# A first norm summed by token, x fetched first, and two of the last four token groups scaled on GpSimd

## The reference, cut to what matters

```python
h = jnp.concatenate([meta, x], axis=1)                 # 528 x 1024
xn = rmsnorm(h, g_mix_pre[l])                          # h * rsqrt(mean(h*h) + 1e-6) * g
proj = xn @ w_in[l]                                    # columns: q, k, v, r, a_low, u, z_gla, z_ssm
...
log_a = jax.nn.log_sigmoid(a_low @ w_gate_up[l] + b_gate[l]) / GATE_TAU
...                                                    # gated linear attention, state-space layer, FFN
...                                                    # second block: attention, convolution, mixture of experts
x = x + gt2 * hierarchical_moe(...)
return rmsnorm_2(x, final_norm_g)                      # 512 x 1024, the output
```

## Time and profile before

| | |
|---|---|
| median of 3 runs | 1752.39 us (1750.7 to 1757.69) |
| the profiled execution's own time | 1752.41 us |
| its span | 1750.6 us |
| TensorE matmul busy | 1661.9 us, 95% |
| VectorE busy | 1192.2 us, 68% |
| ScalarE busy | 736.7 us, 42% |
| GpSimd busy | 329.5 us, 19% |
| granted TensorE clock, mean | 0.979 |

### The profile page before, as it was taken

One profiled execution on the slowest core, in us unless ns is written; L12 is line 12 of the kernel. 1 busy time (PEld: TensorE's weight loads), 2 busy tenths in 40 slices (PEclk: granted clock), 3 DMA queues, 4 the chain that ended last, 5 costly groups with the idle time before them and its releaser, 6 DMA issues.

```text
span 1750.6 us, 20019 instructions
## 1 busy us (share of the span) xinstructions
PE 1661.9 (95%) x8290; PEld 1328.2 (76%) x8290; DVE 1192.2 (68%) x1584; ACT 736.7 (42%) x975; POOL 329.5 (19%) x191
## 2 busy tenths in 40 slices
PE   6999899899999998999999998999999998999997
PEld 4878787777888886888887897878755776777775
DVE  5979768872434337953466446968965657899998
ACT  5253445444422243221222224334476237677774
POOL 1000011214100001600000000433401004355452
PEclk8999999999999998999999998999999999999999
DMA  5535213433322233444334421222210105999995
GB/s 221 187 116 168 71 61 111 138 110 109 121 96 94 91 131 118 168 168 176 135 146 170 157 107 56 108 83 97 97 48 1 72 1 222 383 387 383 385 364 188
DMA packets 59643, 264.54 MB, mean 151 GB/s; under 512 B 21648, under 2 KB 22288, under 8 KB 33056
## 3 DMA queue, kind: packets, MB, share of 16 engines
q1 hardware_dynamic: 34896, 159.10, 24.9%
q0 software_dynamic: 15184, 99.90, 14.5%
q10 hardware_dynamic: 9472, 4.26, 0.9%
HBM read 239.80 MB, written 23.44 MB: 150 GB/s over the span
## 4 chain that ended last, share of the span: by engine, by line
PE 73%; DVE 17%; ACT 6%; DMA 2%; issue 1%; POOL 1%; ACTq 0%; SPq 0%; DVEq 0%; POOLq 0%
PE bank L377 72%; DVE bank L2378 3%; DVE wsplit L1699 2%; DVE wsplit L2644 2%; DMA ring<-in_wmoe,indices 1%; ACT wsplit L1049 1%; DVE parts L2644 1%; ACT parts L1636 1%; DVE products_early L1795 1%; POOL wsplit L1699 1%; DVE block_out L2686 0%; DVE x_in L1726 0%; PE bank L854 0%; DMA x_in<-in_xT 0%; DVE products_early L1814 0%
## 5 line engine op out<-in xcount | busy, mean ns | idle before, releaser
L377 PE MATMUL bank<-h_high,wsplit 128*128 128x512 f32 (+1 forms) x1056 | 329.1, 391 | 11.4 <-DVE h_low L2221 4.9
L1699 DVE TENSOR_TENSOR wsplit<-ring,wsplit 128x2048 fp32r<-128x2048 f32 x77 | 178.8, 2322 | 158.5 <-ACT wsplit L1049 158.3
L1049 ACT ACTIVATE wsplit<-ring 128x2048 fp32r<-128x2048 f32 x98 | 187.1, 1909 | 202.0 <-PE bank L377 190.8
L377 PEld LDWEIGHTS bank<-h_high,wsplit 128*128 128x128 f32 x1056 | 199.9, 193 | 55.1 <-DVE h_low L2313 5.4
L377 PE MATMUL bank<-xn_high,wsplit 128*128 128x512 f32 (+1 forms) x832 | 220.1, 352 | 11.0 <-DVE xn_low L1730 8.1
L377 PE MATMUL bank<-h_low,wsplit 128*128 128x512 f32 (+1 forms) x528 | 204.5, 387 | 0.0
L377 PEld LDWEIGHTS bank<-xn_high,wsplit 128*128 128x128 f32 x832 | 147.4, 193 | 33.9 <-DVE xn_low L1730 8.1
L377 PE MATMUL bank<-f_high,wsplit 128*128 128x512 f32 (+1 forms) x576 | 171.8, 375 | 1.1 <-DVE wsplit L1699 1.1
L377 PE MATMUL bank<-xn_low,wsplit 128*128 128x512 f32 (+1 forms) x416 | 144.9, 348 | 0.0
L1699 POOL TENSOR_TENSOR wsplit<-ring,wsplit 128x2048 fp32r<-128x2048 f32 x21 | 97.4, 4640 | 176.8 <-ACT wsplit L1049 176.7
L377 PEld LDWEIGHTS bank<-f_high,wsplit 128*128 128x128 f32 x576 | 105.3, 188 | 21.1 <-DVE wsplit L1699 1.3
(11 more groups left out here) (508 smaller groups left out, 3309.3 us busy)
## 6 DMA issues: line engine op xcount, KB each, us to landing
ring<-in_W SPq DMA_DIRECT2D x122, 1024.0 KB, 4.8
weights_out<-prep SPq DMA_DIRECT2D x8, 864.0 KB, 5.5
prep<-weights_out_early POOLq DMA_DIRECT2D x8, 576.0 KB, 3.1
xslot<-zeros SPq DMA_DIRECT2D x7, 516.0 KB, 5.1
block<-xslot SPq DMA_DIRECT2D x6, 516.0 KB, 12.0
yslot<-block_out SPq DMA_DIRECT2D x6, 512.0 KB, 8.7
prep<-turns_early POOLq DMA_DIRECT2D x8, 288.0 KB, 2.4
x_in<-in_xT SPq DMA_DIRECT2D x4, 528.0 KB, 7.5
```

The source lines that it names most:

```text
L377: return g.matmul(o, l, r, start=first, stop=last_, skip_group_check=True)
L1049: g.activation(wst[:, side(n), 0, :], ringt[:, n % RING, :], ACT.Copy).then_inc(*a.sig(("high", n)))
L1699: g.tensor_tensor(wst[:, side(n), 1, :], ringt[:, n % RING, :], hi, SUB).then_inc(*t.sig(("low", n), ("released", n)))
```

## The change

The x loads are issued first, then the constants, ring load 0, the vectors, ring load 1, `wal`, `wgu`, ring load 2. The squares are summed over k on VectorE; TensorE then sums over the partitions with the squares as the stationary operand, so that the sum of a token lies on one partition: 128x5 instead of 128x528. Root and reciprocal are taken of that small tile, and TensorE spreads it again into two PSUM banks, from which the scaling reads it. Small products (`keep_busy`) stand before, between and behind. The first weight unit is split in two halves, its low part by VectorE and GpSimd; the second unit's high part goes between the x parts on ScalarE and its low part directly behind the scaling loop on VectorE. The root's table is loaded at the start. At the end, groups 0 and 1 are scaled on GpSimd in two steps.

```diff
 tensor:
+            def keep_busy(n):
+                for _ in range(n):
+                    t = mm(idle[:, 0:128], ones, ident, True, True)
+                t.then_inc(*p.sig(("free", "idle")))
             p.wait_ge(cst_landed, 16)
-            for k in range(8):
-                p.wait_ge(*at("sq", k))
-                mm(ba, ones, sq[:, k % 4, 0:512], k == 0, k == 7)
-                mm(bb[:, 0:16], ones, sq[:, k % 4, 512:NT], k == 0, k == 7)...
+            keep_busy(4)
+            b = fresh("ms")
+            p.wait_ge(*at("ms", "square"))
+            for m, lo in enumerate((0, 128, 256, 384, 400)):
+                t = mm(b[:, m:m + 1], sq[:, 0, lo:lo + 128], ones[:, 0:1], m == 0, m == 4)
+            t.then_inc(*p.sig(("ms",)))
+            keep_busy(2)
+            b, b2 = fresh("ms", "scale"), fresh("ms", "tail")
+            p.wait_ge(*at("inverse", "ms"))
+            for m in range(4):
+                mm(b[:, 128 * m:128 * m + 128], rt5[:, m:m + 1].to_broadcast([128, 128]), ident, True, True)
+            mm(b2[:, 0:16], rt5[:, 4:5].to_broadcast([128, 128]), ident[:, 112:128], True, True)...
+            keep_busy(8)
 linear:
-                p.wait_ge(*at("low", n))
+                p.wait_ge(*at("low_part", 0) if n == 0 else at("low", n))
+                        if n == 0 and k == 4:
+                            p.wait_ge(*at("low_part", 1))
 scalar:
+            g.activation(small[:, 40:41], small[:, 40:41], ACT.Sqrt)          # loads the table
-                    a.wait_ge(*at("summed", k - 4))
-                g.activation(sq[:, k % 4, :], HT0[:, k, :], ACT.Square)...
-            high(0)
-            root(("ms", 1), rst[:, 512:NT], 1024, 16)
-            root(("ms", 0), rst[:, 0:512], 1024, 512)
+                    a.wait_ge(*at("sq_added", k - 3))
+                g.activation(sq[:, 1 + (k - 1) % 3 if k else 0, :], HT0[:, k, :], ACT.Square)...
+            g.activation(rt5, banks.at("ms")[:, 0:5], ACT.Sqrt, scale=1.0 / 1024, bias=eps)...
+            high_part(0, 0)
+            high_part(0, 1)
             for k in range(8):
                 g.activation(xnh[:, k, :], HT0[:, k, :], ACT.Copy)...
+                if k in (3, 5):
+                    high_part(1, k // 4)
-            next_high("k", 0)
 vector:
-            low(v, g, 0)
-            inverse(rst[:, 512:NT], "root", "ms", 1)
-            inverse(rst[:, 0:512], "root", "ms", 0)
+            for k in range(1, 8):
+                v.wait_ge(*at("sq", k))
+                g.tensor_tensor(sq[:, 0, :], sq[:, 0, :], sq[:, 1 + (k - 1) % 3, :], ADD)...
+            g.reciprocal(rt5, rt5)...
+            low_part(v, g, 0, 0)
             for k in range(9):
-                    g.scalar_tensor_tensor(out=HT0[:, k, :], in0=HT0[:, k, :], ..., in1=rst, ...)
+                    for w, c in (("scale", slice(0, 512)), ("tail", slice(512, NT))):
+                        g.scalar_tensor_tensor(out=HT0[:, k, c], in0=HT0[:, k, c], ...,
+                                               in1=banks.at("ms", w)[:, 0:c.stop - c.start], ...)
+            next_low("k", 0)                     # was behind ssm_angle
 finish(m):
                 g.reciprocal(ss[:, 4 + m:5 + m], ss[:, m:m + 1]).then_inc(*v.sig(("y_inverse", m)))
+                if m < 2:
+                    return
 gpsimd:
+            low_part(q, g, 0, 1)                 # ahead of the odd x parts
+            for m in range(2):                   # at the very end
+                q.wait_ge(*at("y_inverse", m))
+                g.tensor_scalar(HT[:, m, 0:1024], HT[:, m, 0:1024], ss[:, 4 + m:5 + m], None, MUL)...
+                q.wait_ge(*q.own())
+                g.tensor_tensor(HT[:, m, 0:1024], HT[:, m, 0:1024], ROWS[:, 1, :], MUL)...
 sync:
-            g.dma_start(vt[:, :], vecs)...; g.dma_start(ct[:, :], cst[:, 0:NCST])...
             for i in range(4):
                 g.dma_start(HT0[:, 2 * i:2 * i + 2, :], xT[:, 2 * i:2 * i + 2, :])...
+            g.dma_start(ct[:, :], cst[:, 0:NCST])...
+            load(0)
+            g.dma_start(vt[:, :], vecs)...
+            load(1)
             g.dma_start(walt, wal)...
             g.dma_start(wgut[0:16, :], wgu)...
-            loads(0, RING)
+            load(2)
```

More of the change, by code:

```diff
@@ L264, in program @@
         rx, z4 = small[:, 16:20], small[:, 20:24]
-        rt4 = small[:, 44:48]
+        rt4, rt5 = small[:, 44:48], small[:, 48:53]
         hh, hl = tile("h_high", 0, 8, 512, dt=F32R), tile("h_low", 14336, 8, 512, dt=F32R)
@@ L1075, in root, with high_part @@
                 g.activation(o, b[:, 0:w], ACT.Sqrt, scale=1.0 / dim, bias=eps).then_inc(*a.sig(("free", *name), ("root", *name)))
+            def high_part(n, z):
+                w = slice(1024 * z, 1024 * z + 1024)
+                a.wait_ge(*landed(n))
+                g.activation(wst[:, side(n), 0, w], ringt[:, n % RING, w], ACT.Copy).then_inc(*a.sig(("high_part", n, z), ("high", n)))
+            a.wait_ge(*at("one"))
+            g.activation(small[:, 40:41], small[:, 40:41], ACT.Sqrt).then_inc(*a.sig())
             for k in range(8):
@@ L1080, in scalar @@
                 if k > 3:
-                    a.wait_ge(*at("summed", k - 4))
-                g.activation(sq[:, k % 4, :], HT0[:, k, :], ACT.Square).then_inc(*a.sig(("sq", k)))
-            high(0)
+                    a.wait_ge(*at("sq_added", k - 3))
+                g.activation(sq[:, 1 + (k - 1) % 3 if k else 0, :], HT0[:, k, :], ACT.Square).then_inc(*a.sig(("sq", k)))
             a.wait_ge(cst_landed, 16)
-            root(("ms", 1), rst[:, 512:NT], 1024, 16)
-            root(("ms", 0), rst[:, 0:512], 1024, 512)
+            a.wait_ge(*at("ms"))
+            g.activation(rt5, banks.at("ms")[:, 0:5], ACT.Sqrt, scale=1.0 / 1024, bias=eps).then_inc(*a.sig(("free", "ms"), ("root", "ms")))
+            high_part(0, 0)
+            high_part(0, 1)
             for k in range(8):
@@ L1715, in scaled @@
                 g.scalar_tensor_tensor(out=o, in0=x, scalar=gain, in1=rs, op0=MUL, op1=MUL).then_inc(*v.sig((name, k)))
-            low(v, g, 0)
-            inverse(rst[:, 512:NT], "root", "ms", 1)
-            inverse(rst[:, 0:512], "root", "ms", 0)
+            g.memset(small[:, 40:41], 1.0).then_inc(*v.sig(("one",)))
+            for k in range(1, 8):
+                v.wait_ge(*at("sq", k))
+                v.wait_ge(*v.own())
+                g.tensor_tensor(sq[:, 0, :], sq[:, 0, :], sq[:, 1 + (k - 1) % 3, :], ADD).then_inc(*v.sig(("sq_added", k), ("ms", "square")))
+            v.wait_ge(*at("root", "ms"))
+            g.reciprocal(rt5, rt5).then_inc(*v.sig(("inverse", "ms")))
+            low_part(v, g, 0, 0)
             v.wait_ge(vecs_landed, 16)
-            v.wait_ge(*v.own())
+            for k in range(4):
+                v.wait_ge(x_landed[k], 16)
+            v.wait_ge(*at("ms", "scale"))
             for k in range(9):
                 if k < 8:
-                    v.wait_ge(x_landed[k // 2], 16)
-                    g.scalar_tensor_tensor(out=HT0[:, k, :], in0=HT0[:, k, :], scalar=vec("g_mix_pre")[:, k:k + 1], in1=rst,
-                                           op0=MUL, op1=MUL).then_inc(*v.sig(("xn_value", k)))
+                    for w, c in (("scale", slice(0, 512)), ("tail", slice(512, NT))):
+                        g.scalar_tensor_tensor(out=HT0[:, k, c], in0=HT0[:, k, c], scalar=vec("g_mix_pre")[:, k:k + 1],
+                                               in1=banks.at("ms", w)[:, 0:c.stop - c.start], op0=MUL, op1=MUL).then_inc(
+                            *v.sig(("xn_value", k), ("free", "ms", w)))
                 if k % 2:
@@ L1824, in vector @@
             g.tensor_scalar(q1, q1, PI_IN, -PI_IN, ALU.min, MAX).then_inc(*v.sig(("ssm_angle",)))
-            next_low("k", 0)
             v.wait_ge(*at("ssm_abs"))
```

29 lines of the change are left out of this document (21 added, 8 removed).

## The result

The changed kernel is slower, where I had forecast 5.7 us faster: 1759.57 us median (22 runs, 1748.41 to 1765.84) against 1753.09 for the kernel before (22 runs, 1749.81 to 1759.53). The ratio is 1.0036, 95% interval 1.0025 to 1.0047: some 6 us slower.

What follows compares the result with a forecast made beforehand. Bound: mostly TensorE, with a latency chain in front of its dense stretch. Span 1750.6 - 9.3 (front) + 3.6 (tail) = 1744.9; time 1752.4 - 5.7 = 1746.7 us, range 1741.5 to 1752.5, forecast chance 0.45.

Steps and rivals of the forecast that it cites:

- The front, -9.3: Kernel start up to the gates: earlier x, smaller norm and faster scaling gain 9.3 us, between 6.6 and 10.8.
- the pair of k without GpSimd's interference: Scaling loop: with the scale read from PSUM, VectorE stops waiting for GpSimd's split; a pair takes 2.45 us instead of 3.04.
- TensorE's wait of 1.3 us: At the gates, TensorE, 10.8 us early, waits about 1.5 us for banks VectorE frees, 8.0 early with 1.3 slack.
- my fear for the clock level: Front, TensorE: less sure that the granted level has risen from 0.50 by 20 us; staying low costs 3.0 us.
- From 110 on everything 9 us early: After the front, unchanged code to the tail: the 9.3 us gained in front are kept throughout.
- The tail, +3.6: Last 12 us: finishing groups 0 and 1 on GpSimd delays the final stores, losing 3.6 us, between 1.4 and 4.4.
- The one-operand multiply of 128x1024: Tail, GpSimd: one of two steps per group, taken as 1.05 us, between a copy's 1.0 and the two-operand 2.3.
- Three stores after group 1, 5.6 us: Tail, SP: stores go in group order, so three start only after group 1; the end comes 5.6 us later.
- Rival (4): Tail: contention slows GpSimd's products to 6.5 us each, delaying three stores; 1755.2 us, slower than before; chance 0.08.
- (1): Tail and gate banks: GpSimd gets the port first twice, banks free early enough; -10.8 + 1.4, 1743.0 us; chance 0.24.
- (2): Front, TensorE: small products do not lift the clock, first 6 us at 1.2 GHz; 7.4 early, 1748.6 us; chance 0.13.
- (3): Front, loads: x lands no earlier, at 12.2, as transfers share engines; front gains 6.6, 1749.4 us; chance 0.10.

Runs made afterwards that it cites:

- the five unpadded kernels with the new front: Kernels whose TensorE program is that of the change, without extra 1x1 products; state-space stage averages 445.9 us, against 441.8 with the old front.
- the front alone: The change with the last four groups finished on VectorE as in the kernel before; 1750.59 us, ratio 0.9977, and 1747.71 us, 0.9973, when repeated.
- the front alone with shifted code: New front, old tail, with 16, 32 or 48 extra 1x1 TensorE products, or 13 keep-busy products removed; ratios 0.9950, 0.9939 (repeated 0.9934), 0.9949, 0.9948.

## Why the prediction was wrong

**The front, -9.3: right, in part by luck.** x, the scale at 16.7, the pair of k without GpSimd's interference, VectorE's 9.5 (I had 8.0) and TensorE's wait of 1.3 us all came as written. The measured shift is 9.1 us at 44 and 9.7 at 186 us. The wait came out right because two errors cancelled: at the gates VectorE is 8.8 us early (forecast 8.0) and TensorE 12.1 (forecast 10.8). Small errors: the constants land at 9.5 (10.7 forecast), and my fear for the clock level was needless even without the idle products. With all but one of them gone the first 60 us read

```profile
0.00:60.00 60.00, 46.25 (x301) 42.84 (x302) 45.16 (x152) 25.33 (x42) 10.95 (x11) 1.00 0.68 260
```

level 1.00 throughout, and the kernel is 9.1 us early at 43.8 all the same.

**"From 110 on everything 9 us early": wrong.** I carried 9.3 us over 1600 us of unchanged code. In the state-space stage the five unpadded kernels with the new front lose 445.9 - 441.8 = 4.1 us, to 3 us more gaps and to the low level behind them. 9.3 - 4.1 is 5.2, the front alone measured 4 (0.9977 and 0.9973). That the loss does not come from the work of the front is shown by the front alone with shifted code, whose ratios of 0.9934 to 0.9950 are 9 to 12 us.

**The tail, +3.6: the step that failed.** It measured +9.8 alone. Its lower end should read 1.5 (1752.1 - 1750.6), not 1.4, which changes nothing. Three terms, by the trace of after:
- The one-operand multiply of 128x1024 was priced at 1.05 us, near the copy. It takes 2.85 beside VectorE's additions from PSUM, which keep their pace (1.48 us for two), more than the two-operand product, 2.34. Two of them add 3.6 us to the GpSimd chain; the collisions gave some 1.2 back, since one multiply was stretched by 0.95 where the value taken had 2.1 for both. Group 1 was ready 11.7 us after the first reciprocal started instead of 9.3: 2.4 us.
- Three stores after group 1, 5.6 us: right, 1742.3 to 1747.7 is 5.4.
- The end of the program: no term at all in the sum. It comes 9.2 us after GpSimd's last instruction, not 5.6: 3.6 us.
The forecast's 3.6 with these two additions of 2.4 and 3.6 is 9.6.

The Trainium skill ("VectorE: DVE Perf Modes", "The DRAIN you can't avoid") says that the DRAINs which the runtime puts before and behind a program take a constant 12 ns or so on all five engines. The closing DRAINs here stand at a line of the kernel itself, and no run shows whether that sentence means them. Taken for them the figure would be far off: they took 9120 to 18063 ns on GpSimd in the three traces shown, 6260 on TensorE and 324 on ScalarE, and one of them set the end. The port rule of the Trainium skill ("SBUF — State Buffer", the notes under its diagram of the port sides), quoted in the prediction, holds for the one-operand multiply in so far as it and VectorE's scaling stretched each other, 3.8 and 1.95 us. That one of them holds the ports to its end this trace does not show: the scaling started 1.2 us into the multiply (1737.24 and 1736.03) and ended 0.65 us before it (1739.19 and 1739.84).

**The rivals.** Rival (4) had the right side and the right place, GpSimd in the tail, but another mechanism: contention on every product, of which there was little. (1) failed on the same multiply, and the bank was binding, by 1.3 us. (2) and (3) did not occur: level 1.00, x landing in 4.9 us in the median. The total fits the measured terms: -9.3 + 4.1 + 9.8 = +4.6, measured +6 with an interval of 4.4 to 8.2.

**The better kernel** is the front with the old tail and TensorE's code moved: 1739.7 and 1743.5 us in two comparisons, ratios 0.9939 and 0.9934, against 1.0036 for the change.

## What to carry to other kernels

Before moving work to an engine that had finished early, read the instructions that close the program on each engine: their end is a second critical path, and GpSimd's trails its last instruction by 9 us. A gain at the front is only a gain at the end if the stages between keep their own waits: measure the shift at several lines, in more than one profile. When adding a few instructions changes a far stage, shift the code by dummy instructions in an idle place before explaining the difference by the work.

## What the runs showed of the hardware

- GpSimd's DRAIN at the end of the program is over 9.0 us after its last instruction, be that a product of 2.34 us, a memset of 0.1 or the issue of an indirect transfer (over at 1725.1 in the trace of before, DRAIN until 1734.1).
- On GpSimd a multiply of 128x1024 by a per-partition scalar (2.85 us) is slower than the product of two tiles of that size (2.34).
- Of 24 issues by SyncE that met the start of a 16 KB piece of TensorE's code, 21 took 0.66 to 1.61 us instead of 0.32 or 0.43, and where this met the load at 355 us its 864 KB landed after 7.6 to 7.9 us instead of 5.7 to 6.3. Shifting the code by 32 idle products was worth 6.9 +- 1.1 us of 1750, 0.4%, as much as this whole change.
- Profiled executions of one kernel differ by 5 to 6 us (the change: 1753.3 and 1758.0 us; the front alone: 1753.6 and 1747.7), mostly in the time at 0.50 in the state-space stage (10.2 and 17.1 us; 27.3 and 17.1), which costs half of itself. The first profile of the change was a lucky one; alone it would have said that the front keeps its 9 us (8.8 at 1735 us, 4.0 in the second).
